# Compression with a 60-column operand, and a bias table read in long runs

## The reference

```python
cmp_idx = np.arange(n_cmp)[:, None] * NSA_CMP_STRIDE + np.arange(NSA_CMP_BLOCK)[None, :]
def compress(raw, pos, w1, w2):                       # once for keys, once for values
    blocks = raw.reshape(B, S_pad, G, HEAD_DIM)[:, cmp_idx] + pos[:, None, :]
    blocks = blocks.transpose(0, 3, 1, 2, 4).reshape(B, G, n_cmp, NSA_CMP_BLOCK * HEAD_DIM)
    return jax.nn.silu(blocks @ w1) @ w2              # w1 is 2048 x 256, w2 is 256 x 64
```

## Time and profile before

| | |
|---|---|
| median of 3 runs | 1184.1 us (1184.07 to 1189.37) |
| profiled execution, its own time | 1183.93 us |
| span from first to last instruction | 1182.1 us |
| PE busy | 1168.1 us, 99% |
| DVE busy | 832.0 us, 70% |
| ACT busy | 667.8 us, 56% |
| granted PE clock, mean share | 0.998 |
| weights through SP's queue | 200.60 MB |

### The profile page before, as it was taken

One profiled execution on the slowest core, in us unless ns is written; L12 is line 12 of the kernel. 1 busy time (PEld: TensorE's weight loads), 2 busy tenths in 40 slices (PEclk: granted clock), 3 DMA queues, 4 the chain that ended last, 5 costly groups with the idle time before them and its releaser, 6 DMA issues.

```text
span 1182.1 us, 18521 instructions
## 1 busy us (share of the span) xinstructions
PE 1168.1 (99%) x7432; PEld 1023.1 (87%) x7432; DVE 832.0 (70%) x1260; ACT 667.8 (56%) x1085; POOL 219.2 (19%) x287
## 2 busy tenths in 40 slices
PE   8999999999999999999999999999999999999997
PEld 7986788888898788888888888899998699888886
DVE  6868777766568687766667877547977877777753
ACT  6538666643443666665446555546655865655642
POOL 0106442110000341111111111110001931111201
PEclk9999999999999999999999999999999999999999
DMA  8891245565457235455544554554453123555552
GB/s 304 276 229 38 108 181 202 187 213 194 148 195 285 73 138 182 179 184 208 214 177 148 199 188 162 189 197 164 170 207 138 60 93 131 188 178 181 185 193 82
DMA packets 33654, 206.05 MB, mean 174 GB/s; under 512 B 3856, under 2 KB 6432, under 8 KB 11808
## 3 DMA queue, kind: packets, MB, share of 16 engines
q1 hardware_dynamic: 29840, 200.60, 47.3%
q10 hardware_dynamic: 3728, 4.26, 1.8%
HBM read 203.39 MB, written 1.46 MB: 173 GB/s over the span
## 4 chain that ended last, share of the span: by engine, by line
PE 87%; DMA 4%; DVE 4%; ACT 3%; POOL 1%; issue 1%; ACTq 1%; DVEq 0%; POOLq 0%; SPq 0%
PE ps L684 40%; PE ps L689 21%; PE ps L701 3%; PE ps L702 3%; PE ps L703 3%; PE ps L2057 2%; PE ps L2059 2%; PE ps L2058 2%; DMA e_bt<-scratch 2%; DMA raw<-wstream 2%; DVE wl L632 1%; ACT wh L603 1%; PE ps L1015 1%; DMA h<-xt 1%; PE ps L715 1%
## 5 line engine op out<-in xcount | busy, mean ns | idle before, releaser
L632 DVE TENSOR_TENSOR wl<-raw,wh 128x2048 fp32r<-128x2048 f32 (+4 forms) x190 | 417.8, 2205 | 100.4 <-ACT wh L603 100.4
L603 ACT ACTIVATE wh<-raw 128x2048 fp32r<-128x2048 f32 (+2 forms) x192 | 351.0, 1832 | 123.6 <-PE ps L689 57.9
L684 PE MATMUL ps<-xb,wh 128*128 128x512 f32 x1392 | 333.6, 392 | 0.0
L684 PEld LDWEIGHTS ps<-xb,wh 128*128 128x128 f32 x1392 | 255.7, 188 | 51.0 <-issue 0.8
L684 PE MATMUL ps<-ab,wh 128*128 128x512 f32 x772 | 188.3, 392 | 0.6 <-DVE ab L1081 0.6
L689 PEld LDWEIGHTS ps<-xb,wl 128*128 128x128 f32 x1392 | 178.4, 191 | 6.8
L689 PE MATMUL ps<-xb,wl 128*128 128x256 f32 x1392 | 180.5, 283 | 0.0
L684 PEld LDWEIGHTS ps<-ab,wh 128*128 128x128 f32 x772 | 140.6, 188 | 28.1 <-DVE ab L1081 1.5
L940 DVE TENSOR_TENSOR tf<-ps,tf 128x256 f32<-128x256 f32 x148 | 62.4, 424 | 102.9 <-ACT tf L935 102.9
L935 ACT ACTIVATE tf<-ps 128x256 f32<-128x256 f32 x148 | 56.5, 384 | 121.0 <-PE ps L689 120.7
L689 PEld LDWEIGHTS ps<-ab,wl 128*128 128x128 f32 x772 | 101.1, 191 | 5.1
(11 more groups left out here) (375 smaller groups left out, 1724.1 us busy)
## 6 DMA issues: line engine op xcount, KB each, us to landing
raw<-wstream SPq DMA_DIRECT2D x168, 1024.0 KB, 4.8
raw<-wstream SPq DMA_DIRECT2D x16, 704.0 KB, 4.2
raw<-wstream SPq DMA_DIRECT2D x4, 792.0 KB, 4.4
raw<-wstream SPq DMA_DIRECT2D x4, 512.0 KB, 6.8
e_bt<-scratch ACTq DMA_DIRECT2D x16, 128.0 KB, 8.3
o_bt<-scratch SPq DMA_DIRECT2D x2, 1024.0 KB, 5.7
raw<-wstream SPq DMA_DIRECT2D x2, 560.0 KB, 8.7
raw<-wstream SPq DMA_DIRECT2D x2, 528.0 KB, 3.4
```

The costliest lines, as they stand in the source:

```text
L603: e.g.activation(WH[i % HLN][:, 0:w], RAW[i % RAWN][:, 0:w], ACT.Copy).then_inc(S["hi"], 1)
L632: e.g.tensor_tensor(WL[q][:, 0:w], RAW[i % RAWN][:, 0:w], f32(WH[q][:, 0:w]), ALU.subtract).then_inc(S["lo"], 1)
L684: e.g.matmul(two(PS[p.bank[p.unit(n)]][:, :]), WH[c % HLN][:, at * 128:at * 128 + 128], x2[:, :, tile(ks[k])], start=k == 0, stop=False, s ...
```

## The change

1. `plan()` and `gemms()`: the chunks now come as 5, 6 `cmpk`; 7, 8 `qn`; 9, 10 `cmpv`; 11 `ks`. PE's order is `km`, `cmpk`, `qn`, `cmpv`, `ks`, `hs`, three steps of `ev0`, `kc`, `vc`, the rest of `ev0`.
2. High and low half of a slice stand side by side in `e_blk`, so that one operand of 60 columns holds both. Two matmuls take the place of three: 60 columns by the high half of w1, 60 by its low half. The result has 60 rows (it now also contains low x low).
3. ACT copies the 60 rows out of PSUM (`hidden`). `hs` becomes four matmuls with a 60 x 30 matrix `e_fold` of two stacked identities, which transposes and adds the two halves. POOL makes it at the start. Silu comes behind `hs`, once, on 128 partitions x 120 columns.
4. The rows in DRAM are laid out so that eight heads follow one another; a DMA of `spread_bias` has 16 runs of 2944 numbers (11,776 bytes), one for each partition, which carry 128 unused numbers between heads. `e_bt` grows from 16 to 23 KB a partition. Its part for heads 0 to 7 lies over `e_blk`. ACT issues heads 8 to 15 behind its work for `qn` (now chunk 10), and heads 0 to 7 behind the copy out of `cmpv`.

```diff
-    for name in ("cmp_k_w1", "cmp_v_w1"):
-        toks(name, 0, 0, 256, range(16), 8)
+    toks("cmp_k_w1", 0, 0, 256, range(16), 8)
     cols("even_w_in", 0, [[(1536 + 64 * j, 64), (1536 + 64 * (4 + j), 64)] for j in range(4)], k8, 16)
+    toks("cmp_v_w1", 0, 0, 256, range(16), 8)
...
+        e_bt = place("e_bt", 2 * 2944, at=list(rl))
+        rl[0] += 16 * 1024
+        e_fold = place("e_fold", 30, at=m)
+        e_blk = place("e_blk", 4 * 480, F32R, at=rl)
...
             for a in range(8):
-                src = bass.AP(scratch.tensor, 8 * half * 16 * 385 + 127 - 16 * a, [[384, 16], [16 * 385, 8], [1, 256]])
-                e.g.dma_start(e_bt[16 * a:16 * a + 16, hs].rearrange("p (h s) -> p h s", h=8), src).then_inc(S[f"bt{half}"], 16)
+                src = bass.AP(scratch.tensor, 8 * half * 384 + 128 - 16 * a, [[16 * 384, 16], [1, 7 * 384 + 256]])
+                e.g.dma_start(e_bt[16 * a:16 * a + 16, hs], src).then_inc(S[f"bt{half}"], 16)
...
+        halves_of = e_blk[:, :].rearrange("p (i m a n) -> p i m a n", i=2, m=16, a=2)
+        def bt_at(h):
+            return (2944 if h < 8 else 0) + h % 8 * 384
...
         def pool_even(e):
+            e.wait_ge(S["d_c"], 16)
+            ident = c_("ident")
+            e.g.tensor_tensor(e_fold[0:60, :], ident[0:60, 0:30], ident[0:60, 30:60], ALU.add).then_inc(S["fold"], 1)
...
-            e.g.dma_start(bass.AP(scratch.tensor, 0, [[16 * 385, 16], [385, 16], [1, 384]]),
+            e.g.dma_start(bass.AP(scratch.tensor, 1, [[384, 16], [16 * 384 + 1, 16], [1, 384]]),
...
+            def hidden(i, p):
+                def drain(e, _):
+                    e.wait_ge(*p.end[0])
+                    e.g.activation(e_hs[i][0:60, :], PS[p.bank[0]][0:60, 0:256], ACT.Copy).then_inc(S["ev_act"], 1)
+                return drain
+            act_gemm(e, G["cmpk"], drain=hidden(0, G["cmpk"]))
             act_gemm(e, G["qn"])
             spread_bias(e, 1)
-            act_gemm(e, G["ks"])
+            act_gemm(e, G["cmpv"], drain=hidden(1, G["cmpv"]))
             spread_bias(e, 0)
+            act_gemm(e, G["ks"], ahead=1)
+            e.wait_ge(*G["hs"].end[0])
+            e.g.activation(e_hz[:, 0:120], PS[G["hs"].bank[0]][:, 0:120], ACT.Exp, scale=-1.0).then_inc(S["cz"], 1)
...
+            dve_gemm(e, G["cmpk"], 0)
             dve_gemm(e, G["qn"], 0, drain=dve_to(G["qn"], e_qn, 0, by=1))
+            dve_gemm(e, G["cmpv"], 0)
+            dve_gemm(e, G["ks"], 0, drain=dve_to(G["ks"], e_ks, 0), ahead=1)
+            e.wait_ge(S["cz"], 1)
+            e.link(e.g.tensor_scalar(hz, hz, 1.0, None, ALU.add))
+            e.settle()
+            e.link(e.g.reciprocal(hz, hz))
+            e.settle()
+            e.g.tensor_tensor(e_ht[:, :], o[:, 0:60], hz[:, 0:60], ALU.mult)
...
+                    ins = e.g.tensor_tensor(hrv[:, jb, g, :, 0:15], o[:, c:c + 15].unsqueeze(1).broadcast_to([128, 4, 15]),
+                                            hz[:, c:c + 15].unsqueeze(1).broadcast_to([128, 4, 15]), ALU.mult)
...
+            lo_to(e, G["ev0"].first + 1)
...
-                    e.g.matmul(o, e_blkh[:, s], wh[:, sl], start=mi == 0, stop=False)
-                    e.g.matmul(o, e_blkl[:, s], wh[:, sl], start=False, stop=False)
-                    ins = e.g.matmul(o, e_blkh[:, s], wl[:, sl], start=False, stop=mi == 15)
+                    sl, both = slice(at * 256, at * 256 + 256), halves_of[:, i, mi, :, :]
+                    e.g.matmul(o, both, wh[:, sl], start=mi == 0, stop=False)
+                    ins = e.g.matmul(o, both, wl[:, sl], start=False, stop=mi == 15)
...
+            e.wait_ge(S["fold"], 1)
-                    ins = e.g.transpose(o[:, c:c + 30], e_hs[i][0:30, jb * 128:jb * 128 + 128], c_("ident")[0:30, 0:30])
+                    ins = e.g.matmul(o[:, c:c + 30], e_hs[i][0:60, jb * 128:jb * 128 + 128], e_fold[0:60, :], start=True,
+                                     stop=True)
```

More of the change, by code:

```diff
@@ L295, in gemms @@
         Gemm("qm", "cols", 4, 8, 16, "ev_dve", wide=True), Gemm("km", "cols", 4, 8, 16, "ev_dve", fixed=(4,)),
-        Gemm("cmpk", "line", 1, 16, 8, "ev_dve"), Gemm("cmpv", "line", 1, 16, 8, "ev_dve"),
+        Gemm("cmpk", "line", 1, 16, 8, "ev_act"),
         Gemm("qn", "cols", 4, 8, 16, "ev_dve", wide=True),
+        Gemm("cmpv", "line", 1, 16, 8, "ev_act"),
+        Gemm("ks", "cols", 2, 8, 16, "ev_dve", fixed=(3, 4), wide=True),
         Gemm("hs", "small", 1, 0, 0, "ev_dve"),
-        Gemm("ks", "cols", 2, 8, 16, "ev_dve", fixed=(3, 4), wide=True),
         Gemm("kc", "small", 1, 0, 0, "ev_dve", fixed=(0,)), Gemm("vc", "small", 1, 0, 0, "ev_dve", fixed=(1,)),
@@ L397 @@
 SEMS = ("fsum dga dgp iw smv er ct0 ct1 gated iv ptd rl eps psa psb pss pr ysq ysum acc adt ah al blk blkh blkl bt0 bt1 const cq cts cum cva cvd cz d_c d_out d_scr d_v ea "
[L398 removed]
+        "ev_act ev_dve fold rel low ex fah fal gemm gp gq gs gz h_down0 h_down1 h_eo h_oo hi lam_a lam_d lf lo mh ml mx na "
         "d_g warm warmed y0 acc0 split d_row ht_a ht_p z0 z1 s0 s1 pre fl fy fr o_v o_p fo nb_a nb_m nb_y nrm oa oh ol om pa pce pcm pcs pct pcx pg pmm pn_v psq pt ptc pv py q0 q1 q2 q3 r ra "
@@ L1193, in pool_even @@
                 for g in range(2):
-                    bv = blk[i][:, 0:480].rearrange("p (m n) -> p m n", m=16)[:, :, g * 15:g * 15 + 15]
+                    bv = windows(i)[:, :, g * 15:g * 15 + 15]
                     s = 2 * i + g
@@ L1226, in act_even @@
             for i in range(2):
-                sl = slice(i * 480, i * 480 + 480)
                 e.wait_ge(S["blk"], i + 1)
-                e.g.activation(e_blkh[:, sl], blk[i][:, 0:480], ACT.Copy).then_inc(S["blkh"], 1)
+                e.g.activation(halves_of[:, i, :, 0, :], windows(i), ACT.Copy).then_inc(S["blkh"], 1)
             e.wait_ge(S["row"], 1)
             row = TMP[1][0:16, 0:384]
-            e.g.dma_start(bass.AP(scratch.tensor, 0, [[16 * 385, 16], [385, 16], [1, 384]]),
+            e.g.dma_start(bass.AP(scratch.tensor, 1, [[384, 16], [16 * 384 + 1, 16], [1, 384]]),
                           bass.AP(row.tensor, row.offset, [list(row.ap[0]), [0, 16], [1, 384]])).then_inc(S["d_scr"], 16)
             act_gemm(e, G["km"])
[L1235 to L1241, removed]
+            def hidden(i, p):
[4 more added lines that the diff above has]
+            act_gemm(e, G["cmpk"], drain=hidden(0, G["cmpk"]))
             act_gemm(e, G["qn"])
             spread_bias(e, 1)
-            act_gemm(e, G["ks"])
+            act_gemm(e, G["cmpv"], drain=hidden(1, G["cmpv"]))
             spread_bias(e, 0)
+            act_gemm(e, G["ks"], ahead=1)
+            e.wait_ge(*G["hs"].end[0])
+            e.g.activation(e_hz[:, 0:120], PS[G["hs"].bank[0]][:, 0:120], ACT.Exp, scale=-1.0).then_inc(S["cz"], 1)
             act_gemm(e, G["ev0"], drain=act_toks(G["ev0"], e_v, 0, 0))
@@ L1321, in dve_even @@
             for i in range(2):
-                sl = slice(i * 480, i * 480 + 480)
                 e.wait_ge(S["blkh"], i + 1)
-                e.g.tensor_tensor(e_blkl[:, sl], blk[i][:, 0:480], f32(e_blkh[:, sl]), ALU.subtract).then_inc(S["blkl"], 1)
+                e.g.tensor_tensor(halves_of[:, i, :, 1, :], windows(i), f32(halves_of[:, i, :, 0, :]),
+                                  ALU.subtract).then_inc(S["blkl"], 1)
             lo_to(e, G["cmpk"].first + 1)
[L1326 to L1336, removed]
+            dve_gemm(e, G["km"], 1, drain=dve_to(G["km"], e_km, 0), between=lambda e, c: lo_to(e, G["qn"].first))
+            dve_gemm(e, G["cmpk"], 0)
             dve_gemm(e, G["qn"], 0, drain=dve_to(G["qn"], e_qn, 0, by=1))
+            dve_gemm(e, G["cmpv"], 0)
+            dve_gemm(e, G["ks"], 0, drain=dve_to(G["ks"], e_ks, 0), ahead=1)
             p = G["hs"]
-            o = PS[p.bank[0]]
-            e.wait_ge(*p.end[0])
-            e.g.tensor_copy(e_ht[:, :], o[:, 0:60])
+            o, hz = PS[p.bank[0]], e_hz[:, 0:120]
+            e.wait_ge(S["cz"], 1)
[4 more added lines that the diff above has]
+            e.g.tensor_tensor(e_ht[:, :], o[:, 0:60], hz[:, 0:60], ALU.mult)
             e.wait_ge(S["zero"], 1)
@@ L1461, in pe_even, with hidden @@
             pe_cols(e, G["km"], range(8), XB, x_ready(0))
-            for i, name in enumerate(("cmpk", "cmpv")):
-                p = G[name]
-                o = PS[p.bank[0]][0:30, 0:256]
+            def hidden(i, p):
+                o = PS[p.bank[0]][0:60, 0:256]
                 e.wait(p.free[0])
@@ L1502, in pe_even @@
             ins.then_inc(S["gemm"], 1)
[L1503 to L1506, removed]
             for x in range(4):
                 pe_toks(e, G["ev0"], x_ready(0), slice(3 + x, 4 + x))
+                if x == 0:
+                    e.wait(G["kc"].out[0])
+                    for g in range(2):
+                        e.wait(G[f"cs{g}"].free[0])
                 for n in (2 * x, 2 * x + 1):
```

28 lines of the change are left out of this document (14 added, 14 removed).

## The result

| | before | after |
|---|---|---|
| median of 6 runs each, side by side | 1184.09 us (1183.83 to 1189.37) | 1191.38 us (1189.25 to 1193.36) |
| ratio of the means of the runs | | 1.0052, 95% interval 1.0036 to 1.0068 |
| profiled execution, its own time / span | 1183.93 / 1182.1 us | 1191.65 / 1189.8 us |
| start of the compression to first attention score | 44.64 us | 52.75 us |
| first score to the end of the span | 1098.0 us | 1097.9 us |

The change costs about 7 us, and the span says where: between the compression's first matmul and the first attention score. Behind that the two kernels take the same time.

A forecast was written before the change was run, and what follows sets the result against it. PE was taken as the bound (87% of the chain), with DMA full in this stage. Gains 4.3 - 0.3 + 0.4 = 4.4 us, less 3.7 for chunk 12, took 1183.9 to 1183.2 us; range 1179.0 to 1188.0.

The forecast's parts named there:

- Matmuls, -4.3 us: Compression on PE: 64 matmuls of 0.117 us in place of 96, and no 0.56 us wait; gain 4.3 us.
- `hs`, "no change": PE's step ahead of `ev0`: four small matmuls again, still 0.35 us.
- Silu, +0.3: Chain from `hs` to `kc`: silu newly exposed behind ACT's DMA issues, costing 0.3 us, ends 0 and 0.8.
- attention, -0.4: Behind the first score: an earlier table gives back 0.4 us of PE's 0.47 us idle at 102.98.
- Chunk 12: Weights ahead of `ev0`: wanted by 59.9 us, delayed by the early table half to 63.6, so PE waits 3.7 us.
- the middle of 0.51 and 1.31, 0.91: Price of one 11,776-byte table run in us, seven of which chunk 12 waits for.
- The row alone: Price from the window with table traffic alone: 111 ns per 1000 bytes, 1.31 us a run.
- one for one: Weight and table queues share DMA engines in equal packet counts, read from 115 against 118 packets at 76 to 79 us.
- Rival C: Engines crowd at the same four partitions: 1.50 us a run, chunk 12 at 67.7, PE waits 7.8, 1187.3 us; chance 0.23.
- The two rules: Skill rules: whole packets per queue would land chunk 12 in time; 16 neighbouring partitions on 4 ports speak against the change.
- The later half, "not the bound": Table half issued from 65.9 us: lands at 81.4, ahead of its first use at about 83.9.

The follow-up runs named there:

- e3: The changed kernel with the early table half cut to 64 bytes per partition, heads 8 to 15 using the table of heads 0 to 7: 1180.44 us (0.9962).
- g1: The changed kernel with table runs of 1 KB, a DMA's partitions 8 apart, and the early half issued behind chunk 11's high half: 1180.57 us (0.9955).
- e1: The changed kernel with table runs of 1 KB in place of 11.8 KB, same places and partitions: 1182.55 us (0.9981).
- f2: The kernel before with only the 11.8 KB table runs and their layout, issued at the old places: 1190.94 us (1.0042).
- e2: The changed kernel with each table DMA's 16 partitions 8 apart in place of neighbours, runs still 11.8 KB: 1186.38 us (1.0016).
- f1: The changed kernel with table runs of 1 KB and each DMA's 16 partitions 8 apart: 1181.39 us (0.9966).

## Why the prediction was wrong

- **Matmuls, -4.3 us: right.** 64 matmuls 0.117 us apart, 7.57 us, no wait for chunk 8's low half. `qn` as expected.
- **`hs`, "no change": wrong by 0.65 us** (e3: 1.00 against 0.35). In after it hid under the wait for chunk 12. It also holds the best version at 3.5 us ahead to the first score, where the sum had 4.0.
- **Silu, +0.3, and attention, -0.4: no fault found.** The reciprocal took 0.90 us (0.82 worked out). In e3 and g1 nothing waits for silu. The first maximum no longer waits for the table, but from the first score to the end before and after differ by 0.1 us, and in g1 PE still idles 0.44 us at 99.1: the 0.4 did not come.
- **Chunk 12, the step that failed: its landing, 63.6 forecast, 69.0 measured.** The mechanism was the one forecast: the early half beside chunk 12, ACT and DVE behind it, PE waiting. PE's idle time stood ahead of `hs`, and not ahead of `ev0`, because of ACT's order of work, but `ev0` did start when chunk 12's low half was done, at 73.31 where the forecast had 64.1 + 3.7 = 67.8. Three parts of the price were wrong. The run: "the middle of 0.51 and 1.31, 0.91" was 1.39 us in 53 to 57 us and 0.89 in 57 to 67. The row alone was the right one for a stretch in which only table moves, and such a stretch came, because "one for one" was wrong as well: 39 runs beside 8 packets of weights from 53 to 57 us, and 811 beside 14 in e1. Equal counts in one window of before were taken for a law. Last, a row of weights itself took 0.63 us in the mixture, not 0.33: 8 x 0.30 = 2.4 us for chunk 12 that the formula did not have. In the mean of 16 engines that makes 39 / 16 x 1.39 = 3.4, 65 / 16 x 0.89 = 3.6 and 2.4 us; the 24 runs outside these windows, 1.5 an engine at 0.9 to 1.4, add 1.4 to 2.1: 10.8 to 11.5 us of the measured 12.3 (17.39 - 5.08). This sum is an estimate, since a chunk lands with its slowest engine and not with the mean. By the queues 1.23 + 0.49 = 1.72 MB of weights went from 57 us to the landing, and chunk 12 is 1.05 MB: some engines were well into the next chunks while the slowest still had chunk 12 to do. That the three prices were wrong is shown; how they share the 12.3 us is not.
- **The clock, a term that was missing.** The half clock behind the wait moved the first score by 3.07 us. With it the sum closes: 69.0 - 63.6 = 5.4, and 3.1, on the forecast 1183.2 give 1191.7, against the profiled execution's 1191.65. The rest (0.3 for silu and 0.4 of the attention that did not come, a start 0.3 us earlier) nearly cancels.
- **Rival C** had the nearest landing (67.7), but by runs of 1.50 us one for one, which is not what happened. Its wait of 7.8 us looks like the measured 7.74 and is another quantity: counted as C counts, landing less 59.9, after's wait is 9.1. That 1187.3 and the 4.07 us of half clock add up to the measured 1191.4 is luck.
- **The two rules.** By the Trainium skill's rule of whole packets ("DMA: Bandwidth & Descriptors", section Queues, rings and completion order), read as one run and then chunk 12's eight rows, chunk 12 would have landed in time; the trace is against that reading, 69.0. That 16 neighbours stay slow whatever the length holds: 1.31 us a run against 0.90 spread.
- **The later half, "not the bound": right in after.** It landed at 84.5 us in place of 81.4, later than the first use that was forecast (83.9), and did no harm because the first maximum was only at 92.95. In f2, with the first score at 83.98, the maximum waited for it until 95.17.

Why the long runs cost more than 128 of 1 KB in all: 11.5 KB a partition in place of 8, 1.44 times the bytes, at a price per byte that is no lower (1.31 us / 11.776 = 111 ns per 1000 bytes, as the earlier trace rows have it for 1 KB). There was nothing owed to each packet to be saved. But the bytes are only half of it. A half of the table has 8 x 1.31 = 10.5 us of its own in long runs and 7.5 in short ones, 3.0 apart, while chunk 12 was 12.3 us late behind the one (after) and 6.1 behind the other (e1). Where the other 3.2 us come from is open: no run has long runs with the bytes of the short ones.

## What to carry to other kernels

A transfer's price per byte has to be measured for its own shape in the trace, and a longer run that carries unused bytes is dearer unless a row shows that short ones cost extra. Where weights stream at a DMA share near 1, a small transfer issued in between can delay the next chunk by about its own time and not by its turn (6.1 us for 7.5 in e1, 12.3 for 10.5 in after): cut its bytes first, and put it behind a chunk with slack. Add the half clock behind any forecast PE wait of several us as a term of its own, and count it only from where PE itself, and not a late operand, sets the time.

## What was not expected of the hardware

Weights nearly stand still while small table transfers are queued (14 packets beside 811 in 5 us). A row of 8 KB takes 0.63 us in place of 0.33 beside them. A transfer of 11.8 KB runs costs 75 ns per 1000 bytes even over all 128 partitions, where rows of weights cost 44. And the granted clock fell with a short wait, too: in e2, with PE waits of 2.17 and 0.18 us, it stood at 0.50 from 65.68 to 72.50 us, while in f1, with 0.18 and 0.97 us, it was whole from 60 to 75.
